# Layer norm statistics of a convolution kept as columns, and two more taps on TensorE

## The reference, cut to what matters

```python
def layer_norm(x, g, b):
    mu = jnp.mean(xf, axis=-1, keepdims=True)
    var = jnp.mean(jnp.square(xf - mu), axis=-1, keepdims=True)
    y = (xf - mu) * lax.rsqrt(var + EPS)
    return y * g + b

u = h @ w_in + b_in
a, gate = jnp.split(u, 2, axis=-1)
u = a * jax.nn.sigmoid(gate)
u = conv(u, w_dw, width 31, causal, one filter for each channel) + b_dw
u = jax.nn.silu(layer_norm(u, ln_g, ln_b))
return u @ w_out + b_out
```

## Time and profile before

| | us |
|---|---|
| median of 3 runs | 2198.59 |
| lowest and highest of them | 2196.92, 2199.18 |
| the profiled execution | 2196.72 |
| its span, first to last instruction | 2195.0 |

### The profile page before, as it was taken

One profiled execution on the slowest core, in us unless ns is written; L12 is line 12 of the kernel. 1 busy time (PEld: TensorE's weight loads), 2 busy tenths in 40 slices (PEclk: granted clock), 3 DMA queues, 4 the chain that ended last, 5 costly groups with the idle time before them and its releaser, 6 DMA issues.

```text
span 2195.0 us, 32555 instructions
## 1 busy us (share of the span) xinstructions
PE 2180.3 (99%) x13040; PEld 1933.0 (88%) x13040; DVE 1406.7 (64%) x1315; ACT 992.3 (45%) x821; POOL 202.8 (9%) x105
## 2 busy tenths in 40 slices
PE   8999999999999999999999999999999999999998
PEld 8999888888888888888888898888888888888887
DVE  6999786555555655556767677675555555555655
ACT  6666554443344433444364444554443344433444
POOL 7999000000000000000000000000000000000000
PEclk9999999999999999999999999999999999999999
DMA  9665456555555565655544435555555555555562
GB/s 248 183 175 168 142 191 224 179 198 187 187 176 202 173 209 178 210 172 187 192 159 154 150 115 196 202 181 194 189 190 192 185 198 176 200 187 188 174 210 77
DMA packets 250044, 400.48 MB, mean 182 GB/s; under 512 B 6407, under 2 KB 72143, under 8 KB 249935
## 3 DMA queue, kind: packets, MB, share of 16 engines
q1 hardware_dynamic: 249406, 398.74, 54.7%
q0 software_dynamic: 352, 0.56, 0.1%
q10 hardware_dynamic: 208, 0.07, 0.0%
HBM read 397.24 MB, written 2.10 MB: 182 GB/s over the span
## 4 chain that ended last, share of the span: by engine, by line
PE 92%; DVE 4%; issue 2%; DVEq 1%; DMA 0%; ACT 0%; SPq 0%; ACTq 0%
PE bank L1263 54%; PE bank L1265 28%; PE bank L1539 4%; DVE bank L928 2%; PE bank L1336 2%; PE bank L1524 1%; PE bank L1601 1%; DVEq L906 0%; PE bank L1350 0%; DMA x_rows<-in_x 0%; DVE bank L922 0%; PE bank L1353 0%; DVE bank L909 0%; PE bank L1471 0%; PE bank L1504 0%
## 5 line engine op out<-in xcount | busy, mean ns | idle before, releaser
L1263 PE MATMUL bank<-x_both,w_hi 128*128 128x512 f32 x3328 | 1155.6, 393 | 0.0
L771 DVE TENSOR_TENSOR w_lo<-raw,w_hi 128x2048 fp32r<-128x2048 f32 x343 | 779.1, 2290 | 527.2 <-ACT w_hi L486 527.0
L486 ACT ACTIVATE w_hi<-raw 128x2048 fp32r<-128x2048 f32 x374 | 707.5, 1910 | 625.9 <-PE bank L1265 599.4
L1265 PE MATMUL bank<-x_both,w_lo 128*128 128x256 f32 x3328 | 927.0, 279 | 0.0
L1263 PEld LDWEIGHTS bank<-x_both,w_hi 128*128 128x128 f32 x3328 | 623.2, 187 | 141.1 <-issue 0.3
L1263 PE MATMUL bank<-h_both,w_hi 128*128 128x512 f32 x1872 | 649.4, 392 | 0.4 <-DVE h_both L972 0.4
L1265 PEld LDWEIGHTS bank<-x_both,w_lo 128*128 128x128 f32 x3328 | 627.0, 188 | 0.1
L1265 PE MATMUL bank<-h_both,w_lo 128*128 128x256 f32 x1872 | 521.4, 279 | 0.0
L1263 PEld LDWEIGHTS bank<-h_both,w_hi 128*128 128x128 f32 x1872 | 350.5, 187 | 79.5 <-issue 0.5
L1265 PEld LDWEIGHTS bank<-h_both,w_lo 128*128 128x128 f32 x1872 | 352.7, 188 | 0.0
L1336 PE MATMUL bank<-x_both,w_hi 128*128 128x256 f32 x960 | 173.2, 283 | 0.0
(11 more groups left out here) (216 smaller groups left out, 1183.2 us busy)
## 6 DMA issues: line engine op xcount, KB each, us to landing
raw<-in_ffn_w_gate_up SPq DMA_DIRECT2D x176, 1024.0 KB, 5.0
raw<-in_ffn_w_down SPq DMA_DIRECT2D x88, 1024.0 KB, 5.1
raw<-in_gla_w_in SPq DMA_DIRECT2D x48, 1024.0 KB, 5.2
raw<-in_conv_w_in SPq DMA_DIRECT2D x32, 1024.0 KB, 6.2
raw<-in_conv_w_out SPq DMA_DIRECT2D x16, 1024.0 KB, 5.2
raw<-in_gla_w_out SPq DMA_DIRECT2D x16, 1024.0 KB, 6.6
x_rows<-in_x SPq DMA_DIRECT2D x4, 512.0 KB, 6.2
out<-out_rows SPq DMA_DIRECT2D x4, 512.0 KB, 3.1
```

Of the source, the lines that this page charges most:

```text
L486: nc.scalar.activation(w_hi[k][:, :, :], raw[k][:, :, :], ACT.Copy).then_inc(hi_done, 1)
L771: nc.vector.tensor_tensor(w_lo[k][:, :, :], raw[k][:, :, :], w_hi[k][:, :, :].bitcast(F32), ALU.subtract).then_inc(lo_done, 1)
L1263: mm(to, w_hi[k][:, kt, cols], xx[:, :, k0 + kt, :], start=(first and kt == 0), stop=False, skip_group_check=True)
L1265: ins = mm(to[:, 0:T], w_lo[k][:, kt, cols], xx[:, 0, k0 + kt, :], start=False, stop=(last and kt == 3), skip_group_check=True)
```

## The change

The matmuls for sums swap their operands: the tile becomes the stationary operand, in two halves of 128 tokens, and one column of ones the moving one, so that `y_total` and `sq_total` are 128 x 2. `shift` is no longer added by VectorE; it is one more column sum, with a column of fours. Mean, squared mean, variance, root and reciprocal work on 128 x 2. The negated mean and the reciprocal root are brought back to 128 x 256 by scaling `ident` and multiplying with `ones`, each into two banks of PSUM. VectorE reads the first copies for its first tiles; ScalarE copies the second ones to SBUF (`sq_sum`, `rstd`) for the others. The order on VectorE is: centre tiles 0 and 1, then scale tile 0. Fillers tied to the variance, the root and the reciprocal are gone. `LAST_TAPS` becomes (4, 16), and `join_last(0)` and the adding of ScalarE's taps stand two steps earlier in tile 15.

```diff
-LAST_TAPS = (4, 14)
+LAST_TAPS = (4, 16)
@@ ScalarE
-            nc.scalar.activation(rstd[:, :], rstd[:, :], ACT.Sqrt, bias=eps[:, 0:1]).then_inc(root_done, 1)
+            nc.scalar.activation(ln_cols[:, 2, :], ln_cols[:, 2, :], ACT.Sqrt, bias=eps[:, 0:1]).then_inc(root_done, 1)
+            scalar.wait_ge(rows_done, 2)
+            nc.scalar.activation(sq_sum[:, :], neg_mean_row[1], ACT.Copy).then_inc(rows_kept, 1)
+            scalar.wait_ge(rows_done, 4)
+            nc.scalar.activation(rstd[:, :], rstd_row[1], ACT.Copy).then_inc(rows_kept, 1)
@@ VectorE
-                    if n == JOIN_AT + 4 and last:
+                    if n == JOIN_AT + 2 and last:
...
-            conv_tile(KT // 2 - 1, 1, LAST_TAPS[1], fewer=LAST_TAPS[0], add_at=9, last=True)
+            conv_tile(KT // 2 - 1, 1, LAST_TAPS[1], fewer=LAST_TAPS[0], add_at=7, last=True)
...
+            nm, msq, var, rs = (ln_cols[:, i, :] for i in range(4))
             dve.wait_ge(stat_done, STAT[1] - 1)
-            nc.vector.scalar_tensor_tensor(out=sq_sum[:, :], in0=shift[:, :], scalar=4.0 * P, in1=y_total,
-                                           op0=ALU.mult, op1=ALU.add).then_inc(mean_done, 1)
+            nc.vector.tensor_scalar(nm, y_total, -1.0 / D, None, ALU.mult).then_inc(mean_done, 1)
             dve.wait_ge(mean_done, 1)
-            nc.vector.scalar_tensor_tensor(out=rstd[:, :], in0=sq_sum[:, :], scalar=1.0 / D ** 2, in1=sq_sum[:, :],
-                                           op0=ALU.mult, op1=ALU.mult).then_inc(mean_done, 1)
+            nc.vector.tensor_tensor(msq, nm, nm, ALU.mult).then_inc(mean_done, 1)
             dve.wait_ge(mean_done, 2)
             dve.wait_ge(stat_done, STAT[1])
-            nc.vector.scalar_tensor_tensor(out=rstd[:, :], in0=sq_total, scalar=1.0 / D, in1=rstd[:, :],
+            nc.vector.scalar_tensor_tensor(out=var, in0=sq_total, scalar=1.0 / D, in1=msq,
                                            op0=ALU.mult, op1=ALU.subtract).then_inc(var_done, 1)
+            for a in range(2):
+                ins = nc.vector.tensor_scalar(neg_mean_diag[:, a * P:(a + 1) * P], ident[:, :], nm[:, a:a + 1], None, ALU.mult)
+            ins.then_inc(mean_diag, 1)
+            dve.wait_ge(root_done, 2)
+            nc.vector.reciprocal(rs, var).then_inc(rstd_done, 1)
+            dve.wait_ge(rstd_done, 2)
+            for a in range(2):
+                ins = nc.vector.tensor_scalar(rstd_diag_ln[:, a * P:(a + 1) * P], ident[:, :], rs[:, a:a + 1], None, ALU.mult)
+            ins.then_inc(ln_diag, 1)
...
             ln_center(0)
-            invert(1, rstd[:, :])
+            ln_center(1)
@@ TensorE
+            def column_sums(to, tile, start=False, stop=False, by=None):
+
+                by = ones[:, 0:1] if by is None else by
+                for a in range(2):
+                    ins = mm(to[:, a:a + 1], tile[:, a * P:(a + 1) * P], by, start=(start and a == 0), stop=stop,
+                             skip_group_check=True)
+                return ins
...
-                return mm(sq_total, ones[:, :], square, start=start, stop=stop)
+                return column_sums(sq_total, square, start, stop)
...
-            for signal, count, n in ((var_done, 1, 2), (root_done, 2, 7), (rstd_done, 2, 1), (z_done, 1, 2), (xn_done, KT + 1, 2)):
+            pe.wait_ge(mean_diag, 1)
+            for row in neg_mean_row:
+                mm(row, ones[:, :], neg_mean_diag[:, :], start=True, stop=True).then_inc(rows_done, 1)
+            pe.wait_ge(ln_diag, 1)
+            for row in rstd_row:
+                mm(row, ones[:, :], rstd_diag_ln[:, :], start=True, stop=True).then_inc(rows_done, 1)
+            for signal, count, n in ((z_done, 1, 2), (xn_done, KT + 1, 2)):
```

More of the change, by code:

```diff
@@ L141, in trunk @@
         sq_early = sb("sq_early", [P, 8, T], 72 * K)
-        last_diag = [sb(f"last_diag{j}", [P, P], 80 * K + 512 * j) for j in range(sum(LAST_TAPS))]
-        assert sum(LAST_TAPS) <= 18
+        last_diag = [sb(f"last_diag{j}", [P, P], 80 * K + 512 * j) for j in range(18)]
+        last_diag += [sb(f"last_diag{18 + j}", [P, P], 95 * K + 512 * j) for j in range(2)]
+        assert sum(LAST_TAPS) <= len(last_diag)
+        ln_cols = sb("ln_cols", [P, 4, 2], 93 * K)
+        four = sb("four", [P, 1], 93 * K + 64)
+        neg_mean_diag = sb("neg_mean_diag", [P, T], 91 * K)
+        rstd_diag_ln = sb("rstd_diag_ln", [P, T], 92 * K)
         y_sum = sb("y_sum", [P, T], 69 * K)
@@ L182, in trunk @@
         y_last = [slot[1][:, 2, :], slot[1][:, 0, :]]
-        y_total, sq_total = bank[:, 0, 0:T], bank[:, 1, 0:T]
+        y_total, sq_total = bank[:, 0, 0:2], bank[:, 1, 0:2]
+        neg_mean_row, rstd_row = [bank[:, b, 0:T] for b in (4, 6)], [bank[:, b, 0:T] for b in (5, 7)]
         raw_in = [sem(f"raw_in{i}") for i in range(RING)]
@@ L229, in trunk @@
         var_done = sem("var_done")
+        mean_diag = sem("mean_diag")
+        ln_diag = sem("ln_diag")
+        rows_done = sem("rows_done")
+        rows_kept = sem("rows_kept")
         cent_done = sem("cent_done")
@@ L406, in _ @@
             nc.gpsimd.memset(shift_w[:, :], -1.0 / P).then_inc(consts, 1)
+            nc.gpsimd.memset(four[:, :], 4.0).then_inc(consts, 1)
             for c in range(2):
@@ new lines, in _ @@
+            ins.then_inc(mean_diag, 1)
[5 more added lines that the diff above has]
+            ins.then_inc(ln_diag, 1)
+            def ln_center(t):
+                if t == 0:
+                    dve.wait_ge(rows_done, 1)
+                if t == 3:
+                    dve.wait_ge(rows_kept, 1)
+                nc.vector.tensor_tensor(act[:, t, :], act[:, t, :], neg_mean_row[0] if t < 3 else sq_sum[:, :],
+                                        ALU.add).then_inc(cent_done, 1)
@@ L976, in _ @@
                 dve.wait_ge(cent_done, t + 1)
-                nc.vector.scalar_tensor_tensor(out=act[:, t, :], in0=act[:, t, :], scalar=vcol("ln_g", t), in1=rstd[:, :],
+                if t == 0:
+                    dve.wait_ge(rows_done, 3)
+                if t == 2:
+                    dve.wait_ge(rows_kept, 2)
+                nc.vector.scalar_tensor_tensor(out=act[:, t, :], in0=act[:, t, :], scalar=vcol("ln_g", t),
+                                               in1=rstd_row[0] if t < 2 else rstd[:, :],
                                                op0=ALU.mult, op1=ALU.mult).then_inc(z_done, 1)
-                if t + 1 < KT:
+                if 1 <= t + 1 < KT and t + 1 != 1:
                     ln_center(t + 1)
@@ L1396, in _ @@
             free_slot(0, U_CONV_OUT // 2)
+            def column_sums(to, tile, start=False, stop=False, by=None):
[4 more added lines that the diff above has]
+                return ins
             def add_square(square, signal, count, start=False, stop=False):
                 pe.wait_ge(signal, count)
-                return mm(sq_total, ones[:, :], square, start=start, stop=stop)
+                return column_sums(sq_total, square, start, stop)
             add_square(sq_late[:, 4, :], y_sq, 4, start=True)
             add_square(sq_late[:, 5, :], y_sq, 5)
+            pe.wait_ge(consts, 21)
+            column_sums(y_total, shift, start=True, by=four[:, :])
             pe.wait_ge(ysum_done, KT - 1)
-            mm(y_total, ones[:, :], y_sum[:, :], start=True, stop=False)
+            column_sums(y_total, y_sum)
             for tile in range(2):
```

6 lines of the change are left out of this document (2 added, 4 removed).

## The result

| | us |
|---|---|
| before, median of 17 runs | 2199.06 (2196.88 to 2200.52) |
| after, median of 17 runs | 2203.80 (2202.36 to 2206.64) |
| ratio after / before | 1.0022, 95% interval 1.0016 to 1.0028 |
| span of the profiled execution | 2204.8, before 2195.0 |

The changed kernel is slower by 4.7 us. The time lies inside the stated range, but it is not the forecast's +1.3: it is the second rival, in which TensorE's clock falls. Three executions of the later sessions took far longer than all others (8312.55 of the early Silu alone, 3629.43 and 4400.00 of the kernel before) and are left out of every ratio.

The account below looks back on a forecast made before the run. TensorE, waiting in the gap before the first output product at 224.44, was taken to bound the kernel; +0.24 until the variance and +1.04 from there gave +1.3 us, a median of 2199.9, range 2197.0 to 2204.4.

Parts of the forecast that it names:

- the second rival: TensorE's clock falls to 1.2 GHz in the gap, slowing rows and first output products: +5.8 us, 2204.4; chance 0.16.
- The bound: TensorE's gap from 214.10 to 224.40: the change is worth as many us as it moves the first output product.
- The taps: Tile 15: two taps fewer on VectorE start its last join 0.8 us earlier, but delay TensorE's first sum by 0.84.
- one of its own signs: In the profile after, the prediction is wrong if VectorE's last join in tile 15 moves less than 0.8 us.
- The sums: On TensorE, a column sum costs 0.45 us against 0.42; its queue comes last, so the variance starts 0.24 late.
- The rows and ScalarE's queue: After the variance, Silu's table load waits behind two copies, no longer covered by the reciprocal: +1.04 us to the first output product.
- The drain of 1.38: At ScalarE's table load, a skill page's rule would start Silu 1.38 us later, +2.7 in all; one chance in twenty.
- The range: Total time from 2197.0 (rival 1 and the lower of the runs) to 2204.4 (rival 2).

Follow-up runs that it names:

- early Silu alone: The changed kernel plus a one-column Silu activation straight behind the root, its sums still one column wide; median 2200.85, ratio 1.0005.
- wide sums: The changed kernel with each column sum multiplying 128 columns of ones in place of one, loads and order kept; median 2200.31, ratio 1.0010.

## Why the prediction was right or wrong, point by point

**The bound** held for the stage itself: there the start of the first output product and the clock behind it moved the time. That "nothing behind gives them back or adds to them" did not hold for the profiled execution, to which the fall at 1098 added 3.4 us.

**The taps** held in what they are worth. The first sum started at 215.25 (forecast 215.13), the last join at 216.67 (216.57), and neither the two taps alone nor their removal could be told from no change. By one of its own signs the prediction fails here: the join was to move by at least 0.8 and moved by 0.69. Since TensorE's queue was the last to come, the time doesn't depend on it.

**The sums** held in size, 0.44 each against 0.45, and in who is last. At full clock, in the profile with the early Silu alone, mean and variance start at 219.22 and 219.74; the forecast had 219.28 and 219.74.

**The rows and ScalarE's queue** held: with wide sums the table load came at 223.04 (forecast 222.79), Silu at 224.33 (224.08), the output product at 225.89 (225.72). The load took 1.28 and Silu followed 0.01 behind its end, in the changed kernel too (226.47, 227.76); the drain of 1.38 that the Trainium skill, page "ScalarE: Activation LUTs", section "What ACT_TABLE_LOAD costs", adds did not show in any of these runs. The prediction misread its row on one point: ScalarE was not idle before the load at 215.49, its square ended at 215.47, and in the changed kernel the copy ended at 226.45, 0.02 before the load.

**The step that failed** is that these terms were summed at a granted clock of 1.00, and that the fall was given 0.16. The case spoke of weight loads that "go on without a break for most of the gap" as an argument against it. The wide sums are the counter-proof: the loads stayed as they were, only the columns changed, and the clock held through the sums and the rows. The rival had the mechanism right, and its size by luck: +5.8 was its price, and the profiled pair shows +5.8 at 330 us, but by other shares. The rows at half speed cost 1.8 (4.43 from the variance to the second copy, 2.63 with wide sums), where it said 1.7. But the fall came at 217.7, nearly three microseconds ahead of the 220.43 at which the rival reckoned its cost to begin, so the sums themselves doubled (the mean 1.2 and the variance 1.6 later than with wide sums; the variance 1.9 later than forecast), which the rival had not counted; and the output product ran at half speed for 2.0 us, cost 1.0, where 2.8 was taken. The two errors cancel. Over many runs the change costs 4 to 4.7.

What could have been read ahead: the ten fillers that the change took out. The sum gives their removal no price. Without them the kernel before loses its clock as well, at 222.5 in its profile. They would have pointed to the clock, though not to the sums, where it fell.

**The range** held the time because it was drawn out to the second rival, whose +5.8 was right in sum by luck; the forecast itself, +1.3 with +0.5 to +2.7 around it, did not hold.

## What to carry to other kernels

When TensorE waits for a short chain on other engines, ask of each instruction left in the gap how much it streams, not only whether it is there. A sum against one column costs as much as one against 128 here, 0.44 us a tile either way, and only the wide one kept the clock at 2.4 GHz through sums and rows, in all four of its profiles; in the four with one column it fell during the sums or as they ended.

When a long operation becomes short, look for what ran in its shadow. Here the reciprocal had covered a table load of 1.28 us; a one-column activation ahead of the waiting copies brought it back under cover and gave 2.8 us here, the half-speed stretch that it ended included.

Taking work off an engine that is late by 0.8 us gains nothing if the work goes to the engine that is next: the two taps made no difference that could be measured.

## What the runs showed of the hardware

- The granted clock fell to 0.50 amid one-column matmuls that the page counts as fully busy (216 to 220, 2.00 of 2.00 us), and also within 3.8 us of idling (at 222.5, fillers left out). It came back to 1.00 at 231.4 in the changed kernel, with output products running.
- It fell amid or just behind products with 32 rows (6.8 us at 0.50 in the changed kernel) in six of eleven profiles, none of them of the kernel before itself; with the same products padded with rows of zeros it stayed at 1.00 there in three of three, and the upper part of the spread of the kernel before went away.
- A switch from products of 32 rows to one of 128 shows 0.33 us without any wait that the trace names, at 1090.36, 1091.84 and 1093.31 in the kernel with fillers between the gate's products.
- A weight load of float32 follows another after 0.11 us at 2.4 GHz (216.03 to 216.47 for four) and 0.21 at 1.2 GHz (217.91 to 218.76), so chains of loads feel the clock as streams do.
